# The experts' second weight matrix in two transfers, and its low parts made by two engines

## The reference, cut to what matters

```python
def expert_block(args):
    xb, e = args
    h = jax.nn.silu(xb @ w1[e]) * (xb @ w3[e])      # w1, w3: 1024 x 512
    return h @ w2[e]                                # w2: 512 x 1024
ys = lax.map(expert_block, (xs, block_e)).reshape(n_rows, d) * buf_w[:, None]
out = jnp.zeros((t_tok, d)).at[buf_tok].add(ys)
```

## Time and profile before

| | |
|---|---|
| median of 3 runs (lowest to highest) | 2662.35 us (2657.35 to 2665.19) |
| the profiled execution | 2661.73 us |
| its span in the trace | 2660.0 us |
| busy over the span: PE, DVE, ACT, POOL | 90%, 52%, 41%, 26% |
| mean granted TensorE clock | 0.951 |

### The profile page before, as it was taken

One profiled execution on the slowest core, in us unless ns is written; L12 is line 12 of the kernel. 1 busy time (PEld: TensorE's weight loads), 2 busy tenths in 40 slices (PEclk: granted clock), 3 DMA queues, 4 the chain that ended last, 5 costly groups with the idle time before them and its releaser, 6 DMA issues. The chain is left out here.

```text
span 2660.0 us, 33534 instructions
## 1 busy us (share of the span) xinstructions
PE 2382.1 (90%) x11388; PEld 1862.8 (70%) x11389; DVE 1378.0 (52%) x1958; ACT 1099.6 (41%) x1380; POOL 681.6 (26%) x515
## 2 busy tenths in 40 slices
PE   6779779789999999999999999489999999999990
PEld 5557557568888888888888887367667676667660
DVE  6768464654444344434443444656555554556654
ACT  4423323223333333323333332256556665567653
POOL 4821001000000000000000000186455656458660
PEclk9889889889999999999999999699999999999995
DMA  7744545434345434543463333378778787789877
GB/s 245 288 180 145 190 174 198 159 78 129 99 145 189 128 97 125 204 127 97 123 212 95 99 89 131 118 282 287 243 262 288 272 284 268 257 273 358 286 264 276
DMA packets 311355, 516.29 MB, mean 194 GB/s; under 512 B 32668, under 2 KB 211104, under 8 KB 294880
## 3 DMA queue, kind: packets, MB, share of 16 engines
q1 hardware_dynamic: 294800, 458.17, 49.3%
q0 software_dynamic: 16464, 56.90, 8.6%
HBM read 430.33 MB, written 84.68 MB: 194 GB/s over the span
## 5 line engine op out<-in xcount | busy, mean ns | idle before, releaser
L1492 PE MATMUL mrgps<-xn_hi,w_hi 128*128 128x512 f32 x1024 | 402.0, 393 | 9.0 <-DVE w_lo L1611 9.0
L1492 PE MATMUL mrgps<-xn_lo,w_hi 128*128 128x512 f32 x1024 | 400.3, 391 | 0.0
L1492 PE MATMUL mrgps<-xn_hi,w_lo 128*128 128x512 f32 x1024 | 400.1, 391 | 0.0
L1954 POOL TENSOR_TENSOR w_lo<-w_raw,w_hi 128x1024 fp32r<-128x1024 f32 x128 | 323.0, 2659 | 9.7 <-ACT w_hi L1945 9.7
L1422 ACT ACTIVATE gt<-mrgps,mb 128x512 f32<-128x512 f32 x128 | 88.3, 690 | 505.8 <-PE mrgps L1492 505.8
L1949 DVE TENSOR_TENSOR w_lo<-w_raw,w_hi 128x2048 fp32r<-128x2048 f32 x125 | 286.5, 2355 | 0.1
L1756 POOL IOTA io_g<- 128x4 f32 x1 | 0.1, 144 | 1114.2 <-POOLq L1218 1114.2
L1628 DVE SCALAR_TENSOR_TENSOR tmp<-gt,mrgps 128x512 f32<-128x512 f32 x96 | 66.0, 688 | 389.5 <-PE mrgps L1492 389.5
L686 PE MATMUL mixps<-xn_hi,win_hi 128*128 128x512 f32 x448 | 187.1, 418 | 65.6 <-DVE xn_lo L864 22.4
L1940 ACT ACTIVATE w_hi<-w_raw 128x2048 fp32r<-128x2048 f32 x128 | 239.3, 1919 | 11.1 <-DMA w_raw<-in_expert_w_dram 11.1
L1492 PEld LDWEIGHTS mrgps<-xn_hi,w_hi 128*128 128x128 f32 x1024 | 193.3, 189 | 51.0 <-issue 8.1
(11 more groups left out here) (424 smaller groups left out, 4350.5 us busy)
## 6 DMA issues: line engine op xcount, KB each, us to landing
w_raw<-in_expert_w_dram SPq DMA_DIRECT2D x128, 1024.0 KB, 9.0
w_raw<-in_merge_gate_w_dram SPq DMA_DIRECT2D x128, 512.0 KB, 4.0
w_raw<-in_expert_w_dram SPq DMA_DIRECT2D x32, 2048.0 KB, 11.5
win_hi<-w_in_parts SPq DMA_DIRECT2D x42, 512.0 KB, 3.8
win_lo<-w_in_parts SPq DMA_DIRECT2D x42, 512.0 KB, 5.2
w_raw<-in_branch_w_dram SPq DMA_DIRECT2D x128, 128.0 KB, 4.1
wout<-in_w_out_dram SPq DMA_DIRECT2D x64, 256.0 KB, 4.4
w_raw<-in_x_dram SPq DMA_DIRECT2D x16, 512.0 KB, 10.2
```

Source lines behind the costliest of these rows:

```text
L1492: last = pe.matmul(bank[:], w[:, u % 2, kk], x, start=(kk == w_tiles[0] and j == 0), stop=(kk == w_tiles[-1] and j == 2))
L1954: eng.tensor_tensor(self.lo2[:, f], self.raw2[:, f], self.hi2[:, f].bitcast(F32), ALU.subtract).then_inc(self.split2, 1)
```

## The change

w2's load becomes two DMAs of 1 MB with a semaphore each (`in2[0]`, `in2[1]`), for the rows f = 0, 1 and f = 2, 3. The low parts of f = 0, 1 of the next expert are made by DVE, in `one` behind the low parts of w1 and w3; POOL makes those of f = 2, 3. Each half has its own semaphore of finished low parts (`split2[0]`, `split2[1]`), and SP loads each half once its own low parts are done. For expert 0 POOL still makes all four.

```diff
-    def load2(self, eng, e):
-        eng.dma_start(self.raw2[:], self.io["expert_w2"][0, ds(e, 1)].rearrange("o (k p) n -> p (o k) n", p=P)).then_inc(self.in2, 16)
+    def load2(self, eng, e, half):
+        two = slice(2 * half, 2 * half + 2)
+        eng.dma_start(self.raw2[:, two], self.io["expert_w2"][0, ds(e, 1)].rearrange("o (k p) n -> p (o k) n", p=P)[:, two]).then_inc(self.in2[half], 16)
...
     def write_high2(self, act, e):
-        act.wait_ge(self.in2, e * 16 + 16)
         for f in range(FE):
+            if f % 2 == 0:
+                act.wait_ge(self.in2[f // 2], e * 16 + 16)
             act.activation(self.hi2[:, f], self.raw2[:, f], ACT.Copy).then_inc(self.high2, 1)
...
-    def write_low2(self, eng, e):
-        for f in range(FE):
+    def write_low2(self, eng, e, half):
+        for f in (2 * half, 2 * half + 1):
             eng.wait_ge(self.high2, e * 4 + (f + 1))
-            eng.tensor_tensor(self.lo2[:, f], self.raw2[:, f], self.hi2[:, f].bitcast(F32), ALU.subtract).then_inc(self.split2, 1)
+            eng.tensor_tensor(self.lo2[:, f], self.raw2[:, f], self.hi2[:, f].bitcast(F32), ALU.subtract).then_inc(self.split2[half], 1)
... SP
-                sp.wait_ge(wt.split2, e * 4 + 4)
-                sp.sem_inc(passed, 1)
-                sp.wait_ge(raw_read, blocks * 2 + 1)
-                sp.sem_inc(passed, 1)
-                wt.load2(sp, e + 1)
+                for half in range(2):
+                    sp.wait_ge(wt.split2[half], e * 2 + 2)
+                    sp.sem_inc(passed, 1)
+                    if half == 0:
+                        sp.wait_ge(raw_read, blocks * 2 + 1)
+                        sp.sem_inc(passed, 1)
+                    wt.load2(sp, e + 1, half)
... POOL, in one()
-                    wt.write_low2(pool, pool.snap(e + 1))
+                    wt.write_low2(pool, pool.snap(e + 1), 1)
... DVE, in one(), behind its four write_low13
+                    dve.wait_ge(wt.split2[0], nxt * 2)
+                    dve.sem_inc(passed, 1)
+                    wt.write_low2(dve, nxt, 0)
```

More of the change, by code:

```diff
@@ L1778, in _ @@
                 wt.load13(sp, 0, i)
-            wt.load2(sp, 0)
+            for half in range(2):
+                wt.load2(sp, 0, half)
         @block.scalar
@@ L1918, in __init__ @@
         self.idx_set, self.gathered, self.noted = sem("idx_set"), sem("gathered"), sem("idx_noted")
-        self.in13, self.in2 = [sem(f"w13_in{i}") for i in range(4)], sem("w2_in")
+        self.in13, self.in2 = [sem(f"w13_in{i}") for i in range(4)], [sem(f"w2_in{i}") for i in range(2)]
         self.last13, self.last2 = self.lo13, self.lo2
-        self.high13, self.split13, self.high2, self.split2 = sem("w13_high"), sem("w13_split"), sem("w2_high"), sem("w2_split")
+        self.high13, self.split13, self.high2, self.split2 = sem("w13_high"), sem("w13_split"), sem("w2_high"), [sem(f"w2_split{i}") for i in range(2)]
     def gather(self, pool, dram, column, n):
@@ L2066, in _ @@
             wt.write_low13(pool, 0, 3)
-            wt.write_low2(pool, 0)
+            wt.write_low2(pool, 0, 0)
+            wt.write_low2(pool, 0, 1)
             over_blocks(pool, half_block, one)
@@ L2102, in expand, with contract @@
                     last.then_inc(h_ps, 1)
-            def contract(g, e4):
+            def contract(g, e2):
                 for j in range(2):
@@ L2108, in contract @@
                     for f in two:
-                        pe.wait_ge(wt.split2, e4 + (f + 1))
+                        pe.wait_ge(wt.split2[j], e2 + (f % 2 + 1))
                         for c in range(2):
@@ L2137, in half_contract @@
                     pe.wait_ge(y_free, g * 2 + 3)
-                    pe.wait_ge(wt.in2, e1 * 16)
+                if f % 2 == 0:
+                    pe.wait_ge(wt.in2[f // 2], e1 * 16)
                 if f % 2 == 0:
@@ L2155, in half_block, with one @@
                     half_contract(g, f, e1)
-            def one(g, e4):
+            def one(g, e4, e2):
                 expand(g, e4)
@@ L2162, in one @@
                 turn_h(g, 1)
-                contract(g, e4)
+                contract(g, e2)
             pe.sem_inc(turned, 2)
@@ L2175, in _ @@
                 b1 = pe.value_load(ends[0:1, ds(e + 1, 1)], min_val=1, max_val=NB - 1)
-                e4, e1 = pe.snap(e * 4), pe.snap(e + 1)
+                e4, e2, e1 = pe.snap(e * 4), pe.snap(e * 2), pe.snap(e + 1)
                 final = pe.snap(b1 - 1)
@@ L2180, in _ @@
                         half_block(g, e1)
-                one(final, e4)
+                one(final, e4, e2)
         @block.scalar
```

## The result

| | median us | runs | ratio to before (95% interval) |
|---|---|---|---|
| before, beside it | 2660.55 | 4 | |
| changed kernel | 2777.73 (2775.41 to 2779.39) | 4 | 1.0438 (1.0422 to 1.0455) |

A forecast was written before the change was run, and what follows sets the result against it. PE bounds the kernel, by its standing and clock. With w2 on time, 17 x 39.7 + 12 x 20.35 = 919.1 against 804.31 gives +114.8, plus 3.4 for two more experts: 2780 us, range 2750 to 2815 (76%).

The forecast's parts named there:

- The lateness of w2 goes, -41.6 us: Experts' stage, gate 1 to gate 30: POOL's lighter work lets loads issue earlier, removing all w2 lateness, -41.6 us.
- nothing for PE by itself: Two 1 MB loads of w2 instead of one of 2 MB: same bytes, 0.38 us more on SP's queue, no gain for PE.
- DVE and POOL take turns: At w2's low parts each engine waits for the other's whole instruction: POOL f2, DVE f0, POOL f3, DVE f1, until 24.55.
- first rival: DVE's queued low parts run straight behind w1 and w3's while POOL waits: 2645 us, up to 2670; chance 6%.
- Half blocks, +5.9 us: In experts with a half block, its gate starts at 24.6 instead of 18.73, +5.9 us; PE idles 6.2 us.
- Clock, +2.1 us each: In experts with a half block, PE's clock falls behind 6.2 us of idling: +2.1 us, bounds 1.4 to 3.5.
- Experts without a half block, +1.7: Their next gate starts at 24.6, PE turns h at 25.95 instead of 24.3: +1.7 us per expert.
- Clock in experts without a half block, nothing: The short idling there was taken to leave PE's clock unchanged; bound up to 1.6 us more.
- second rival: POOL slips, so the order is DVE f0, POOL f2, DVE f1: +48.5 us, 2710 us; chance 10%.
- A load of w2 takes 8.4 us at most: Both w2 halves, issued at about 24.6, land by 33.0, before ACT's 34.4, so w2 is on time.
- Sum: Stretch from gate 1 to gate 30: 17 x 39.7 + 12 x 20.35 = 919.1 us against 804.31, +114.8.

The follow-up runs named there:

- two-loads run: Changed kernel without DVE's part: POOL makes all four low parts of w2, one load and semaphore per half; 2631.78 us, 0.9877 of before.
- POOL-waits run: Changed kernel plus one wait: POOL makes its two low parts of w2 only when DVE has made both of its own; 2646.24 us, 0.9928 of before.
- best kernel here that also moved work to DVE: Against the changed kernel, DVE makes f = 2, 3 in the full block using them, POOL f = 0, 1 one block ahead; 2635.13 us.
- with four (2621): Kernel with two loads and all low parts on POOL, changed to four w2 loads of 0.5 MB, a semaphore each; 2620.95 us, 0.9831 of before.
- kernel with DVE's parts in its gap: Changed kernel, but DVE makes f = 0, 1 in the full block using them, around gate-up, where it idled 4.4 us; 2652.34 us.

## Why the prediction was right

- *The lateness of w2 goes, -41.6 us.* Right: ACT waits 0.3 us for w2 in the changed kernel. But the prediction had it from POOL's lighter work and put the split loads at "nothing for PE by itself". That was wrong: the two-loads run leaves all four parts on POOL and wins 29 us with the split alone.
- *DVE and POOL take turns.* Right, to within 0.1 us at each handover of the expert shown, and the POOL-waits run removes the cost by taking only the overlap away. Without the rows of the mixer the sum would have been that of the first rival: DVE's parts alone are worth +1.4 us per half block, not +5.9.
- *Half blocks, +5.9 us.* The gate came at 24.42 instead of 24.6, and PE idled 5.9 us instead of 6.2: the term was 0.2 to 0.3 us too large.
- *Clock, +2.1 us each.* 1.4 and 2.4 in the two rows above. Ten experts follow another one with a half block; from gate to gate they took 38.8 to 40.3 us, 39.4 in the mean, against a forecast of 39.7. Less 31.70 and the gate's 5.7, that leaves 2.0 us for the clock.
- *Experts without a half block, +1.7.* Right: 20.37 us from gate to gate, 20.35 forecast. PE's own recorded wait is 1.31 to 1.35 us of it.
- *Clock in experts without a half block, nothing.* Wrong: behind 7 of the 11 waits of 1.3 to 2.1 us that they brought, the clock did fall. It is these seven in which the second rival came, as the last section shows.
- *The second rival* (DVE's first part goes ahead of POOL) was given 10% as a whole. It came in 9 of the 31 experts, not in all or none. It was also priced too low: its order was POOL's f = 2, then DVE's second part, but both of POOL's went first. From the last low part of w1 and w3 to DVE's second part it took 7.3 us, against 6.6 in the forecast's order and 4.5 in the rival's. Its 2710 us also lie outside the range of 2712 to 2815 that was said to take it in.
- *A load of w2 takes 8.4 us at most.* A misreading without effect: for the last row it was issued at 2080.89 and ACT's high parts began at 2090.68, 9.8 us later.
- *Sum.* The stretch: 919.1 forecast, 920.1 measured. That it fits to 1 us is partly luck, since errors of 2 to 3 us cancel: the experts with a half block took a little less than forecast, and four of those without one took about 21.05 us instead of 20.35, because DVE's part went first.

The Trainium skill (SBUF — State Buffer, section "SBUF: two separate sides") says that of a DVE instruction with two SBUF inputs and a GpSimd instruction that reads SBUF, the one that starts first holds the shared ports for its whole length, and the other is blocked. The trace agrees: a DVE part that takes 1.2 us without POOL beside it is recorded with 3.4 us, and one of POOL's, else 2.35 us, with 3.1 to 3.3.

## What to carry to other kernels

Before work is moved from POOL to an idle-looking DVE, see whether POOL still works at that moment, and whether both read two tensors in SBUF as they do here: then the queue that matters pays for POOL's instructions as well as for its own. Look elsewhere in the trace for a place where both have work queued; it shows the handovers. And when a buffer's reload comes too late, split the load and its semaphore first: with two loads (2632 us) that alone was as fast as the best kernel here that also moved work to DVE (2635), and with four (2621) it was faster.

## What the runs showed of the hardware beyond that

**The turns are not strict.** When DVE's first part got in ahead of POOL, POOL then ran both of its instructions in a row, and DVE's second part waited for both. It did so in 9 of the 31 experts of the changed kernel. Timeline of DVE and POOL in one of them, whose gate is at 2266.57:

```profile
2280.23 1.22 DVE L1957 TENSOR_TENSOR w_lo<-w_raw,w_hi 128x1024 fp32r<-128x1024 f32 x1
...
2281.24 2.93 POOL L1957 TENSOR_TENSOR w_lo<-w_raw,w_hi 128x1024 fp32r<-128x1024 f32 x1
...
2281.36 6.19 DVE L1957 TENSOR_TENSOR w_lo<-w_raw,w_hi 128x1024 fp32r<-128x1024 f32 x1
...
2283.64 2.83 POOL L1957 TENSOR_TENSOR w_lo<-w_raw,w_hi 128x1024 fp32r<-128x1024 f32 x1
```

POOL's second begins 0.53 us before its first is recorded as ended, where in the strict case the records overlap by about 0.03 us. A pair of that kind seems to leave DVE no opening. That is a reading of records, which are rough for POOL; no run here tests it.

Why DVE was first can be read from ACT. Here are its w2 high parts in this expert, and in one (gate at 2547.02) where the turns were strict:

```profile
2277.73 3.90 ACT L1948 ACTIVATE w_hi<-w_raw 128x1024 fp32r<-128x1024 f32 x4
...
2556.89 3.91 ACT L1948 ACTIVATE w_hi<-w_raw 128x1024 fp32r<-128x1024 f32 x4
```

They begin 11.16 and 9.87 us after the gate. POOL needs the third of them, done about 2.9 us later, at 14.1 and 12.8; DVE comes free at 13.7. In all seven experts in which the clock fell behind the short wait, ACT began at 11.0 to 11.2 and DVE went first. In the other two of the nine, POOL was still at the add of rows.

**Short waits can lower the clock.** In full blocks a wait of PE of 1.35 us (L2094 at 2268.01 above) was followed by a stretch at 1.2 GHz, first row. A wait of 1.33 us at the same place, ahead of the second row, was not. Of the nine waits of 1.30 to 1.35 us five were followed by a fall, and both of those of 2.03 and 2.06 us were:

```profile
2268.01:2272.95 4.94, 4.67 (x14) 3.43 (x15) 4.38 (x8) 4.47 (x5) 1.07 (x2) 0.65 0.97 378
2548.46:2555.20 6.74, 6.46 (x28) 5.02 (x29) 6.19 (x9) 6.26 (x6) 1.10 (x2) 1.00 0.99 394
```

In half blocks the waits of about 1.59 us in the POOL-waits kernel were not, in any of 16. Nor does the length of a wait decide there. In the kernel with DVE's parts in its gap, PE restarted behind 2.36 us (first row) and behind 3.25 us (second row), and the clock fell only at the shorter wait:

```profile
1859.85:1873.34 13.49, 13.49 (x56) 8.39 (x57) 2.70 (x6) 3.57 (x8) 5.42 (x6) 0.87 1.01 384
2213.29:2225.17 11.88, 11.88 (x56) 7.64 (x57) 2.71 (x7) 3.46 (x8) 3.64 (x5) 1.00 1.00 395
```

What PE does around the wait differs between the two kinds of block: in a full block the short 128x128 turns of x stand ahead of it, in a half block a dense half expand. What decides was not tried.
